# Splitting q and k in the projection stage of a two-layer transformer trunk, and another order in differential attention

## The reference

```python
def diff_attn_block(q1, q2, k1, k2, v, lam):
    s1 = jnp.einsum('bhqd,bhkd->bhqk', q1, k1) * scale
    s2 = jnp.einsum('bhqd,bhkd->bhqk', q2, k2) * scale
    p = jax.nn.softmax(s1, axis=-1) - lam * jax.nn.softmax(s2, axis=-1)
    return jnp.einsum('bhqk,bhkd->bhqd', p, v)
...
qx = rope_2d(qx); kx = rope_2d(kx)          # the 1024 tokens alone
k1 = jnp.concatenate([kc[0], kx[0]], axis=2) # tokens see context and tokens
ob_x = sweep_query_blocks(lambda q1, q2: diff_attn_block(q1, q2, k1, k2, v_all, lam), qx[0], qx[1])
ob_c = diff_attn_block(qc[0], qc[1], kc[0], kc[1], vc, lam)   # context sees context
```

## Time and profile before

| what | value |
|---|---|
| median of 3 runs | 4222.05 us (4220.51 to 4226.47) |
| profiled execution | 4207.65 us, its span 4206.0 us |
| TensorE busy | 3500.0 us, 83% |
| VectorE busy | 2124.1 us, 51% |
| ScalarE busy | 1261.2 us, 30% |
| GpSimd busy | 223.8 us, 5% |
| mean granted TensorE clock | 0.92 |
| L664 convolution steps, 120 | 188.1 us, 1568 ns each |

### The profile page before, as it was taken

How to read it: one execution, slowest core, us unless ns; L and a number is a source line. 1 busy time by engine, 2 the same in 40 slices (tenths; PEclk the granted TensorE clock), 3 DMA queues, 4 the chain that set the end, 5 groups by cost and what they waited for, 6 DMA issues and landing times. The chain is left out here.

```text
span 4206.0 us, 48006 instructions
## 1 busy us (share of the span) xinstructions
PE 3500.0 (83%) x18199; PEld 2870.6 (68%) x18199; DVE 2124.1 (51%) x2406; ACT 1261.2 (30%) x2015; POOL 223.8 (5%) x335
## 2 busy tenths in 40 slices
PE   2898677739799999999494888888888479999996
PEld 1776455527688888888393767667776468888884
DVE  4598354474434434444452565555556454444445
ACT  2111244353211112111242554444455222111121
POOL 0011000001100000000030000000000010000000
PEclk6899788879899999999696999999999789999998
DMA  4211433223211011100322000000000521111112
GB/s 158 68 60 62 165 136 133 91 90 120 61 40 50 30 35 35 50 30 21 136 87 76 14 12 12 12 12 4 13 5 6 185 81 47 47 56 40 50 50 90
DMA packets 233242, 259.87 MB, mean 62 GB/s; under 512 B 51424, under 2 KB 190400, under 8 KB 232112
## 3 DMA queue, kind: packets, MB, share of 16 engines
q1 hardware_dynamic: 226768, 241.02, 17.6%
q0 software_dynamic: 6368, 17.39, 1.3%
HBM read 217.42 MB, written 40.96 MB: 61 GB/s over the span
## 5 line engine op out<-in xcount | busy, mean ns | idle before, releaser
L1010 DVE TENSOR_TENSOR y_sum<-ffn_down_ps,y_sum 128x512 f32<-128x512 f32 x396 | 271.7, 690 | 253.1 <-PE ffn_down_ps L90 253.1
L88 PE MATMUL ffn_gate_ps<-y_hi,ffn_w_hi 128*128 128x512 f32 (+1 forms) x880 | 326.0, 370 | 31.8 <-DVE ffn_w_lo L971 31.8
L89 PE MATMUL ffn_gate_ps<-y_lo,ffn_w_hi 128*128 128x512 f32 (+1 forms) x880 | 325.5, 370 | 0.0
L90 PE MATMUL ffn_gate_ps<-y_hi,ffn_w_lo 128*128 128x512 f32 (+1 forms) x880 | 325.1, 369 | 0.0
L89 PE MATMUL ffn_val_ps<-y_lo,ffn_w_hi 128*128 128x512 f32 (+1 forms) x880 | 323.9, 368 | 0.0
L88 PE MATMUL ffn_val_ps<-y_hi,ffn_w_hi 128*128 128x512 f32 (+1 forms) x880 | 323.8, 368 | 0.0
L90 PE MATMUL ffn_val_ps<-y_hi,ffn_w_lo 128*128 128x512 f32 (+1 forms) x880 | 323.7, 368 | 0.0
L88 PE MATMUL ffn_down_ps<-ffn_w_hi,ffn_act_hi 128*128 128x512 f32 x792 | 312.1, 394 | 13.2 <-DVE y_sum L1010 6.8
L89 PE MATMUL ffn_down_ps<-ffn_w_lo,ffn_act_hi 128*128 128x512 f32 x792 | 309.6, 391 | 0.0
L90 PE MATMUL ffn_down_ps<-ffn_w_hi,ffn_act_lo 128*128 128x512 f32 x792 | 309.3, 390 | 0.0
L971 DVE TENSOR_TENSOR ffn_w_lo<-ffn_raw,ffn_w_hi 128x1024 fp32r<-128x1024 f32 x132 | 158.0, 1223 | 280.9 <-ACT ffn_w_hi L934 280.9
(11 more groups left out here) (270 smaller groups left out, 7764.6 us busy)
## 6 DMA issues: line engine op xcount, KB each, us to landing
ffn_raw<-in_ffn_w_up SPq DMA_DIRECT2D x88, 512.0 KB, 3.8
da_ada_w<-in_ada_w SPq DMA_DIRECT2D x10, 4096.0 KB, 13.0
ffn_raw<-in_ffn_w_down SPq DMA_DIRECT2D x44, 512.0 KB, 5.6
ab_raw<-in_ab_w_in SPq DMA_DIRECT2D x20, 512.0 KB, 3.7
scratch_x<-out_x SPq DMA_DIRECT2D x18, 512.0 KB, 2.6
mod_ada_w<-in_ada_w SPq DMA_DIRECT2D x4, 2048.0 KB, 11.1
scratch_qk<-ab_qk POOLq DMA_DIRECT2D x8, 640.0 KB, 3.3
da_raw<-scratch_qk SPq DMA_DIRECT2D x8, 640.0 KB, 4.7
```

The costliest lines, as they stand in the source:

```text
L88: pe.matmul(out, a_hi, b_hi, start=first, stop=False)
L89: pe.matmul(out, a_hi, b_lo, start=False, stop=False)
L90: return pe.matmul(out, a_lo, b_hi, start=False, stop=last)
L1010: dve.tensor_tensor(part, down_ps[:, half, :], part, ALU.add).then_inc(s.sum_done, 1)
```

## The change

In the projection, GpSimd splits each finished q or k tile: a copy to qk_hi (fp32r, two buffers), then a subtraction to qk_lo (one buffer), and it stores both, so qk becomes two tensors. It waits for its own copy, for the earlier stores from qk_hi[j], and before the subtraction for the stores of the tile before. qk_free is now signalled by the subtraction. In attention, four loads a head (head(h), on SyncE) replace two loads, the rounding and the subtraction; the scores wait for the loads, and their matmuls are what they were. TensorE's iteration becomes: first group of turned(n), scores(n+2), the other groups, the product at odd n (of the pair that was complete one iteration earlier), the modulation at n % 4 = 2. VectorE's becomes combine(n), maxima(n+1), output, bias add. ScalarE's keeps its order.

```diff
@@ projection, GpSimd, one_turn
                 for j in range(2):
                     n = i * 2 + j
                     pool.wait_ge(s.sum_done.sem, s.sum_done.nth(n))
-                    pool.dma_start(qk[n * P:(n + 1) * P, :], qk_t[:, j, :]).then_inc(qk_stored[j].sem, 16)
-                for j in range(2):
-                    pool.wait_ge(qk_stored[j].sem, qk_stored[j].nth(i))
-                    pool.sem_inc(s.qk_free.sem, 1)
+                    if i:
+                        pool.wait_ge(qk_stored[j].sem, qk_stored[j].nth(i - 1))
+                    pool.tensor_copy(qk_hi[:, j, :], qk_t[:, j, :]).then_inc(s.qk_hi_done.sem, 1)
+                    pool.wait_ge(s.qk_hi_done.sem, s.qk_hi_done.nth(n))
+                    if n:
+                        pool.wait_ge(qk_stored[1 - j].sem, qk_stored[1 - j].nth((n - 1) // 2))
+                    pool.tensor_tensor(qk_lo[:, :], qk_t[:, j, :], qk_hi[:, j, :].bitcast(F32), ALU.subtract)\
+                        .then_inc(s.qk_free.sem, 1)
+                    pool.dma_start(qk[0][n * P:(n + 1) * P, :], qk_hi[:, j, :].bitcast(F32)).then_inc(qk_stored[j].sem, 16)
+                    pool.wait_ge(s.qk_free.sem, s.qk_free.nth(n))
+                    pool.dma_start(qk[1][n * P:(n + 1) * P, :], qk_lo[:, :].bitcast(F32)).then_inc(qk_stored[j].sem, 16)
@@ attention, windows of the modulation and place of the product
-        return g if n % ADA_EVERY == ADA_EVERY - 1 and g < ADA_GROUPS else None
+        return g if n % ADA_EVERY == 2 and g < ADA_GROUPS else None
+
+    def pair_at(n):
+        p = (n - QP - 1) // QP
+        return p if n % QP == 1 and 0 <= p < ALL // QP else None
@@ attention, SyncE
-            def piece(h, n):
-                at = h * PIECES + n
-                if at >= 2:
-                    sp.wait_ge(s.raw_split.sem, at - 1)
-                first = (n * B_HEADS + h) * 2 * B_DIM
-                sp.dma_start(raw[:, n, :], qk[first:first + 2 * B_DIM, :]).then_inc(raw_in[n].sem, 16)
+            def head(h):
+                j, rows = h % 2, B_HEADS * 2 * B_DIM
+                if h >= 2:
+                    sp.wait_ge(s.s2_full.sem, (h - 1) * NU)
+                for dst, part, first in ((q_hi, 0, 0), (k_hi, 0, rows), (q_lo, 1, 0), (k_lo, 1, rows)):
+                    a = first + h * 2 * B_DIM
+                    sp.dma_start(dst[:, j, :].bitcast(F32), qk[part][a:a + 2 * B_DIM, :]).then_inc(qk_in[j].sem, 16)
@@ attention, ScalarE
-            for n in range(PIECES):
-                first_half(0, n)
             exponentials(0)
             for n in range(ALL):
                 if n + 1 < ALL:
                     exponentials(n + 1)
                 turn_copy(n)
-                if split_at(n):
-                    first_half(*split_at(n))
@@ attention, VectorE
             maxima(0)
-            for n in range(ALL + 2):
+            for n in range(ALL + QP + 1):
+                if n < ALL:
+                    combine(n)
                 if n + 1 < ALL:
                     maxima(n + 1)
-                if n % QP == 1 and n > QP:
-                    output(n // QP - 1)
+                if n and pair_at(n - 1) is not None:
+                    output(pair_at(n - 1))
                 if n and window(n - 1) is not None:
                     m.add(dve, window(n - 1))
-                if n < ALL:
-                    combine(n)
-                    if split_at(n):
-                        second_half(*split_at(n))
@@ attention, TensorE
-            for n in range(ALL + 1):
-                if n + 2 < ALL:
-                    scores(n + 2)
-                if n < ALL:
-                    turned(n)
-                if n % QP == 0 and n:
-                    product(n // QP - 1)
+            for n in range(ALL + QP):
+                for at in range(3):
+                    if n < ALL and at < len(groups(n)):
+                        turned(n, at)
+                    if n + 2 < ALL and at == 0:
+                        scores(n + 2)
+                if pair_at(n) is not None:
+                    product(pair_at(n))
```

More of the change, by code:

```diff
@@ L529, in project_conv_diff @@
         part = sb("part", [P, 2, SEQ])
+        qk_hi = sb("qk_hi", [P, 2, T], F32R)
+        qk_lo = sb("qk_lo", [P, T], F32R)
         v_t = sig
@@ L1179, in values @@
                   .then_inc(v_in[h % 2].sem, 16)
-            piece(0, 0)
-            piece(0, 1)
+            head(0)
             sp.dma_start(lam_t[:, :, :].rearrange("p a d -> p (a d)"), row(lam_vecs.rearrange("a d -> (a d)")))\
@@ L1186, in _ @@
             m.load(sp, 0)
-            piece(1, 0)
-            piece(1, 1)
+            head(1)
+            m.load(sp, 1)
             values(1)
-            m.load(sp, 1)
             m.load(sp, 2)
-            piece(2, 0)
-            piece(2, 1)
+            head(2)
             m.load(sp, 3)
@@ L1196, in _ @@
             m.load(sp, 4)
-            piece(3, 0)
-            piece(3, 1)
+            head(3)
             m.load(sp, 5)
@@ L1209, in _ @@
             act.activation(lam_small[:, 2:4], lam_small[:, 0:2], ACT.Exp).then_inc(s.lam_exp.sem, 1)
-            def first_half(h, n):
-                act.wait_ge(raw_in[n].sem, 16 * (h + 1))
-                if h >= 2:
-                    act.wait_ge(s.s2_full.sem, (h - 1) * NU)
-                act.activation((q_hi, k_hi)[n][:, h % 2, :], raw[:, n, :], ACT.Copy).then_inc(s.raw_hi.sem, 1)
             def exponentials(n):
@@ L1267, in _ @@
             dve.wait_ge(s.lam_done.sem, 1)
-            def second_half(h, n):
-                j = h % 2
-                dve.wait_ge(s.raw_hi.sem, h * PIECES + n + 1)
-                dve.tensor_tensor((q_lo, k_lo)[n][:, j, :], raw[:, n, :], (q_hi, k_hi)[n][:, j, :].bitcast(F32),
-                                  ALU.subtract).then_inc(s.raw_split.sem, 1)
             def maxima(n):
@@ L2377, in trunk @@
     conv_out = scratch("conv", A_WIDTH, T)
-    qk = scratch("qk", 4 * B_HEADS * B_DIM, T)
+    qk = [scratch(f"qk_{part}", 4 * B_HEADS * B_DIM, T) for part in ("hi", "lo")]
     v_rows = scratch("v", T, A_WIDTH)
```

45 lines of the change are left out of this document (20 added, 25 removed).

## The result

The changed kernel takes 4174.48 us, the median of 4 runs (4157.43 to 4180.19), against 4221.28 for 4 runs of the kernel before: a ratio of 0.9883 with an interval of 0.9851 to 0.9915. The profiled execution is the fastest of them, 4157.43 us (span 4155.8).

The account below looks back on a forecast made before the run. VectorE's queue was taken to bound each projection turn, and scores, two maxima and second exponential attention's 7.12 us loop. Projection +33 and attention -52 sum to -19 us: 4203 us against the median of 4222.05, range 4180 to 4234.

Parts of the forecast that it names:

- Rival C: Projection: GpSimd waits behind the unbroken convolution steps instead of stopping them; projection loses 2 us, time 4172 us; chance 0.08.
- part 5: Projection: GpSimd's copies and subtractions stop VectorE for their length, 9.8 us a turn; 33 us lost, bounds 29 and 40.
- part 1: Attention: q and k rounding and subtraction leave six iterations, which saves 24 us.
- The loop of 7.1 us stays: Attention's plain iteration: scores, two maxima and second exponential still set its length, 7.1 us.
- part 2: Attention: first transposes ahead, combine ahead of the maxima, products one iteration later; 16 us saved in sum.
- tail: End of attention: 1 us saved.
- part 3: Attention: of 27 us counted for TensorE's lower clock, a third is regained, 9 us, bounds 0 and 20.
- Rival B: Attention: the denser TensorE queue keeps the clock, so attention gives 65 us, time 4190 us; chance 0.14.
- start, queues and late outputs: Attention: start saves 2 us, bounds 0 and 3; load queues and outputs behind the maxima cost nothing (outputs uncovered: 16).
- rival A: GpSimd's projection split costs 40 us; attention's reordering brings nothing, as late outputs delay combine; time 4236 us; chance 0.16.
- Rival D: Whole kernel: the change cancels, attention gaining 38 us against 35 lost, time 4219 us; chance 0.12.

Follow-up runs that it names:

- e3: The changed kernel without GpSimd's copy and subtraction, the unsplit tile stored twice; 4153.36 us, 0.9849 of the kernel before.
- e9: The changed kernel with GpSimd's subtraction replaced by a second copy, so lo is wrong; 4166.42 us, 0.9876 of the kernel before.
- e2_split: The changed kernel with the old orders of TensorE and VectorE in attention, so only the split's place is changed; 4220.08 us, 1.0003 of the kernel before.
- e6: The changed kernel with scores(n+2) ahead of all transposes of unit n on TensorE; 4188.95 us, 0.9936 of the kernel before.
- e1: The kernel before with the new order of attention alone, q and k still split in attention; 4189.03 us, 0.9927 of the kernel before.
- e7: The changed kernel with products one iteration sooner, at even n, and modulation at n % 4 = 3; 4178.89 us, 0.9913 of the kernel before.
- e4b_other_engines: The changed kernel with ScalarE rounding, VectorE subtracting in place and GpSimd only storing the split; 4160.96 us, 0.9865 of the kernel before.

## Why the prediction was wrong in size and right in direction

**Right: that GpSimd stops VectorE, and that the turn grows by it.** Copies and subtractions enter between back-to-back convolution steps, e3 takes the stretching away, and e9 shrinks it with the instruction's length. The Trainium skill ("SBUF — State Buffer", Who interferes with whom) names the lock of the shared ports as the cause; the rows agree for steps of two SBUF operands against both kinds of GpSimd instruction (4.25 and 2.44 us against 1.57). Rival C, GpSimd waiting behind the unbroken row of steps, is out: it got in at the next boundary each time.

**Mis-sized: the copy, in part 5.** I took 2.0 us between 1.3 and 2.9; it took 1.26. The reason given for the value (nearer to GpSimd's other row halved) pointed the right way and stopped short, and ScalarE's copy was the better row. The blocks were 0.3 us shorter than the instructions as well, so a turn cost 7.1 us and not 9.8, and the three turns 22.9 instead of 29 (2 of them for the cosine product that moved into the third). The last turn cost 5.1 instead of 4, since the copy of tile 7 had not been placed, and one term was missing, 2.1 us of v work, at a lower clock whose cause is open. Together 30.0 against 33, inside the bounds of 29 and 40. That the two agree so well is in part luck: the copies and the blocks were some 8 us too dear, and some 5 us of other terms had been left out.

**Right: the splits, in part 1.** 24 us and a part of the clock were forecast; e2_split gave 26.8, 24.2 of them in the six iterations.

**Wrong: "The loop of 7.1 us stays", in part 2.** This is the step that failed. I had read the plain iteration as scores, two maxima, second exponential. These add up to 2.0 + 2.9 + 1.3 = 6.2 us and not to 7.12, and I had not looked for the 0.9 us in ScalarE's row just ahead of the first exponential, which shows three copies ending as it starts, 0.8 us after its maximum was there. The order takes one of the three out of the loop, and a plain iteration falls to 6.48 us (e2 and e6, without this, stay at 7.11 and 7.18, and e1, with it, is at 6.49). I had also taken the shortest plain iteration for all of them: behind a large product and no split it took 7.68, as combine waited for that product's output, and there the order saves 1.2 us. The same wait for combine, 0.5 us, is in the modulation iterations of e2 (7.93, against 7.46 after), for which I had counted a loss.

Four iterations in a row, plain, product, modulation, product, took 7.68 + 8.95 + 7.93 + 8.95 = 33.5 us in e2_split and take 6.5 + 8.25 + 7.46 + 8.25 = 30.5 in the kernel after: 3.0 us less, where the figures of the forecast give 0.75. The order on top of the splits gave 39.1 us, and 26 were forecast (16, clock 9, tail 1). By the starts of the scores, 20.0 of the 39.1 lie in the thirteen iterations around and behind the short units, where 14 were forecast, 18.5 in the other 26, where the forecast had 2 and its clock, and the rest in the tail. Why the first share is 6 us larger I have not divided.

**Mis-sized: the clock, in part 3.** 15 groups of full scores took over 2.2 us before, 13 in e2_split and 11 after. What the full scores took above 2.0 us went from 21.2 to 17.0 and to 15.0 us: 6.2 in all, a little under the third that was taken, and only 2.0 of them by the order. The matmuls behind them I have not divided. Rival B wanted 65 from attention, which gave 69.4 with its start, but for the wrong reason: it wanted the clock kept, and the clock went only from 0.83 to 0.89.

**Right: start, queues and late outputs.** First load to first scores lost 3.5 us where 2 were forecast (bounds 0 and 3, just outside). That outputs wait behind the maxima costs nothing visible: the product iteration is below the forecast, and e7 shows the products' place to be neutral, with which rival A, whose slower case hung on it, is out. It also needed a GpSimd pair above 5.5 us; the pair is 1.26 + 2.9 = 4.2. Rival D's size of attention gain (38) was too small by 31. Rival C's time, 4172, is the nearest of all to the measured one, by luck: it had the projection at 2 us instead of 30, and kept the forecast's attention.

**The sum** with the terms as measured is 30.0 - 3.5 - 65.9 = -39.4, that is 4168.3 for the execution of 4207.65 and 4182 against the median; the two series gave 4174.48 and 4181.11. Attention gave 69.4 us by the forecast's count (52, upper bound 63). The range ended at 4180 because the loop's length was given no lower bound: even the 63 kept the plain iteration at 7.1 us.

**What the experiments corrected in the reasons.** The two parts are not additive, which neither I nor the rivals had: with the splits left in, the new order would have gained 25 us instead of 39. And the choice of GpSimd for the splits is the costly part of the change: the same arithmetic on ScalarE and VectorE costs 11.8 us, and 2.8 with the cosine product moved too.

## What to carry to other kernels

The length of a loop is known only when its ring is closed row by row and the durations add up to the measured length: here 0.9 us were missing. The row just ahead of each step on its own engine has to be looked at, since another unit's small copies may be the last to end, and more than one iteration of a kind has to be measured. An idle GpSimd is no free engine beside a VectorE that sets the pace: arithmetic there cost VectorE nearly the instruction's whole length, for the subtraction 2.6 us where VectorE itself takes 1.5. Where in-order queues wait for each other in a ring, two parts of a change can be worth 25 us each and 66 together, so each is to be timed with the other in place as well as alone.

## What the runs showed of the hardware

GpSimd rounds 128x1280 float32 to fp32r in 1.26 us, as fast as ScalarE and less than half its own 2.9 us for the subtraction. The Trainium skill ("GPSIMD Engine Reference", 4.1 Engine selection) calls its one-input operations roughly line-rate; these rows agree. A copy of one operand holds VectorE up as well: 0.9 us for each of 1.26 (e9_two_copies).

VectorE's nine steps take 14.40 us with GpSimd quiet and 20.53 with a subtraction, a copy and a subtraction in between; a waiting GpSimd instruction gets in at the next boundary of a row without gaps.

The clock at the start of the v work did not follow the length of TensorE's wait before it: 0.85 over the first 10 us after 16.2 us (before), 0.71 after 19.5 (after), 0.83 after 19.2 (e3_store_only), 0.68 after 13.9 (e4b_other_engines).

A load of 128 weight columns that was asked for behind four stores of q and k reached ScalarE 7.8 us later, behind two 4.9 and 6.8 (the two closest to it in time), behind none 3.8 (e3_store_only, before and after, e4b_other_engines).
